# Down products of the experts in pairs: four 32-column quarters of TensorE, three buffers for down weights

## The chip, the cores and the metric

One core of a Trainium2 chip runs the whole program. The metric is the time of one execution on the device in microseconds. Three runs of the kernel before gave 1543.05, 1545.31 and 1547.57 us; their median is 1545.31 us.

## The reference, cut to what matters

The program is one inference step of a two-layer encoder on 544 rows (512 of a prompt and 32 of a sample), 1024 wide, all in fp32. Each layer is a mixer, which the change leaves alone, and then a mixture of 16 experts with hidden width 512, of which every row uses two:

```
gate = ...                               # (rows, 16), two entries of a row are not zero
for e in range(16):
    hid = silu(x @ w1[e]) * (x @ w3[e])  # up: 1024 -> 512
    y = y + gate[:, e:e+1] * (hid @ w2[e])   # down: 512 -> 1024
```

One expert's w1, w3 and w2 are 2 MiB each, so a layer reads 96 MiB of expert weights.

## The kernel before, in words

Each engine has its own instruction list, written out by hand, and semaphores order them. Per layer the rows are normalised, written to DRAM, and a router makes for every expert a list of its rows, at most 96 (`CAP`). When no expert has more than 96 rows, which is so for these inputs, the branch `own_tokens` runs on all engines:

- POOL gathers an expert's 96 rows from DRAM into one of three buffers (`own_tokens` of POOL, line 1954), three experts ahead.
- TensorE turns them (`turn_rows`, line 986: eight transposes), and DVE copies the turned rows to SBUF with the norm's gain (`own_turned`, line 1746).
- `up` (line 1001) makes both hidden products, for w1 and for w3. A stationary tile here is 64 columns of weights and the moving operand is 96 rows' worth of columns. The two 64-column halves of the array take matmuls in turn (`for o in (0, 64)`), with outputs in partitions 0 to 63 and 64 to 127 of a PSUM bank.
- ACT takes the silu (line 1275), DVE multiplies (line 1754) and writes `ghid`, of which there are two buffers.
- `down` (line 1013) multiplies with w2: the stationary tile is 96 columns of `ghid`, the moving operand 512 columns of w2. Per expert that is 2 halves of the output by 4 chunks of the contraction, 8 matmuls. Both halves of the output take PSUM banks 6 and 7.
- ACT copies both banks to `yrow` (`own_rows`, line 1282) and issues one store of 96 x 1024 to DRAM (line 1285).

An fp32 matmul stands in the trace as two MATMUL records, each with its weight load.

TensorE's order per expert is: turn the next expert's rows, `up` of expert e, `down` of expert e-1. So `down` runs one expert behind, and the last two `down` stand one after the other.

Six slots of 2 MiB hold weights: two each for w1, w3 and w2. SP issues all loads in one order (lines 582 and 592). The w1 and w3 of expert e+2 are asked for when `up` of e is done; w2 of e+2 when `down` of e is done. When the last expert's w2 has been asked for, the loads that belong to the next part (`then`: three slots of the next mixer's weights in layer 0, the final gain in layer 1) follow.

When all 16 results are in DRAM, POOL gathers each row's two results (line 1964), and DVE adds them to the stream with their gates (line 1770).

Of the kernel before, what the change touches and what calls it, by code (L numbers as in the profile page):

```python
# [12 lines left out]
P = 128  # L13
# [15 lines left out]
NE = 16  # L29
CAP = 96  # L30
# [13 lines left out]
SB_K, SB_V, SB_Q = 1, 2, 0  # L44
DF_K, DF_V, DF_Q = 4, 1, 2
OUT_EVEN, OUT_ODD = (0, 4), (0, 4)
W1, W3, W2 = (1, 3), (2, 5), (0, 4)


def tok(t):  # L50
# [182 lines left out]
def stream_kernel(nc, x_prompt, x_sample, cache_pool, cache_dsa_k, cache_dsa_v, cache_idx_k, cache_sb_k,  # L233
# [16 lines left out]
    with ctx:  # L250
# [3 lines left out]
        def sem(name):  # L254
            return ctx.enter_context(nc.semaphore(name))
# [4 lines left out]
        xT = sb("xT", [P, KC, NTOK])  # L260
        slot = sb("slot", [P, 6, 4096])
# [3 lines left out]
        arena = sb("arena", [P, 11040])  # L265
# [85 lines left out]
        xgT = arena[:, 3072:4608].rearrange("p (r k n) -> p r k n", r=2, k=KC)  # L351
        gsilu = arena[:, 4608:4992]
        ghid = arena[:, 5120:5888].rearrange("p (r m n) -> p r m n", r=2, m=4)
        yrow = arena[:, 5888:7936].rearrange("p (r d) -> p r d", r=2)
        first_y = normed[:, :].rearrange("p (t d) -> p t d", t=NT)
        second_y = arena[:, 0:5120].rearrange("p (t d) -> p t d", t=NT)

# [29 lines left out]
        bank = ctx.enter_context(nc.psum_tensor("bank", [P, 8, 512], F32))  # L387
# [16 lines left out]
        krow_in = sem("krow_in")  # L404
        vrow_in = sem("vrow_in")
        w13_in = [[sem(f"{q}_w13_in{l}") for q in ("even", "odd")] for l in range(2)]
        w2_in = [[sem(f"{q}_w2_in{l}") for q in ("even", "odd")] for l in range(2)]
        gfin_in = sem("gfin_in")
        bank_filled = sem("bank_filled")
        bank_read = {"act": sem("bank_read_act"), "dve": sem("bank_read_dve")}  # L410
# [38 lines left out]
        up_done = [sem(f"up_done{l}") for l in range(2)]  # L449
# [1 line left out]
        ghid_done = [sem(f"ghid_done{l}") for l in range(2)]  # L451
        down_done = [sem(f"down_done{l}") for l in range(2)]
        yrow_ready = [sem(f"yrow_ready{l}") for l in range(2)]
        y_stored = [[sem(f"y_stored{l}{r}") for r in range(2)] for l in range(2)]
        picked_in = [[sem(f"picked_in{l}{t}") for t in range(NT)] for l in range(2)]
        h_added = sem("h_added")
        rows_known = sem("rows_known")
# [66 lines left out]
        def _(sp):  # L524
# [60 lines left out]
            def w13_load(l, e, par):  # L585
                for w, s in ((moe_w3, W3), (moe_w1, W1)):
                    w_load(w, s[par], l, e, par)

            def w2_load(l, e, par, first=None):
                if first:  # L590
                    first(W2[par])
                sp.dma_start(slot[:, W2[par], :].rearrange("p (k n) -> p k n", k=4),
                             moe_w2[l, e].rearrange("(k p) n -> p k n", p=P)).then_inc(w2_in[l][par], 16)

            def experts(l, first, then=()):


                first(W3[0])
                w_load(moe_w3, W3[0], l, 0, 0)
                w2_load(l, 0, 0, first)  # L600
                first(W1[0])
                w_load(moe_w1, W1[0], l, 0, 0)
                first(W3[1])
                w_load(moe_w3, W3[1], l, 1, 1)
                full = crowded(sp, l)
                with sp.If(full):
                    first(W1[1])
                    w_load(moe_w1, W1[1], l, 1, 1)
                    w2_load(l, 1, 1, first)
                    with sp.Fori(0, NE // 2 - 1) as i:  # L610
                        for par in range(2):

                            sp.wait_ge(moe_y[l], (2 * i + par + 1) * NT)
                            w13_load(l, 2 * i + 2 + par, par)
                            w2_load(l, 2 * i + 2 + par, par)
                    sp.wait_ge(moe_y[l], NE * NT)
                    for load in then:
                        load()
                with sp.Else():

                    first(W1[1])
                    sp.wait_ge(xg_turned[l], 1)
                    w_load(moe_w1, W1[1], l, 1, 1)
                    w2_load(l, 1, 1, first)
                    def up_weights(e, par):

                        sp.wait_ge(up_done[l], e - 1)
                        w13_load(l, e, par)

                    def down_weights(e, par):  # L630
                        sp.wait_ge(down_done[l], e - 1)
                        w2_load(l, e, par)


                    up_weights(2, 0)
                    with sp.Fori(0, NE // 2 - 2) as i:
                        for par in range(2):
                            up_weights(2 * i + par + 3, 1 - par)
                            down_weights(2 * i + par + 2, par)
                    up_weights(NE - 1, 1)  # L640
                    down_weights(NE - 2, 0)
                    down_weights(NE - 1, 1)

                    sp.wait_ge(up_done[l], NE - 1)
                    for load in then[0:2]:
                        load()
                    sp.wait_ge(down_done[l], NE - 1)
                    for load in then[2:]:
                        load()
                    sp.wait_ge(down_done[l], NE)  # L650

            def mixer_left(layer, mech, freed):

# [71 lines left out]
        def _(pe):  # L725
# [11 lines left out]
            def weights(s, n=KC):  # L737
                return slot[:, s, :].rearrange("p (k n) -> p k n", k=n)
# [264 lines left out]
                                                        xgT[:, par, k, :], start=(k == 0), stop=(k == KC - 1))  # L1003
                last.then_inc(up_done[l], 1)

            def down(l, e, par):
                pe.wait_ge(w2_in[l][par], 16 * (e // 2) + 16)
                pe.wait_ge(ghid_done[l], e + 1)
                if e >= 1:
                    pe.wait_ge(yrow_ready[l], e)  # L1010
                for j in range(2):
                    for m in range(4):
                        last = nc.tensor.matmul(bank[0:CAP, 6 + j, :], ghid[:, par, m, :],  # L1013
                                                weights(W2[par], 4)[:, m, 512 * j:512 * j + 512],
                                                start=(m == 0), stop=(m == 3))
                last.then_inc(down_done[l], 1)

            def own_tokens(l):
                turn_rows(l, 0, 0, 0)
                for e in range(NE):  # L1020
                    if e + 1 < NE:
                        turn_rows(l, e + 1, (e + 1) % 3, (e + 1) % 2)
                    up(l, e, e % 2)
                    if e > 0:
                        down(l, e - 1, (e - 1) % 2)
                down(l, NE - 1, (NE - 1) % 2)

            def all_tokens(l):
                with pe.Fori(0, NE // 2) as i:
# [55 lines left out]
        def _(act):  # L1085
# [189 lines left out]
                nc.scalar.activation(gsilu, bank[:, 2 + 2 * (e % 2), 0:4 * CAP], ACT.Silu)\  # L1275
                  .then_inc(gsilu_done[l], 1)

            def own_rows(l, e):
                act.wait_ge(down_done[l], e + 1)
                if e >= 2:  # L1280
                    act.wait_ge(y_stored[l][e % 2], 16 * (e // 2))
                nc.scalar.copy(yrow[0:CAP, e % 2, :].rearrange("p (j n) -> p j n", j=2), bank[0:CAP, 6:8, :])\  # L1282
                  .then_inc(yrow_ready[l], 1)
                act.wait_ge(yrow_ready[l], e + 1)
                act.dma_start(y_dram[l][CAP * e:CAP * e + CAP, :], yrow[0:CAP, e % 2, :])\
                   .then_inc(y_stored[l][e % 2], 16)

            def experts(l):
                full = crowded(act, l)
                with act.If(full):  # L1290
                    all_tokens(l)
                with act.Else():
                    for e in range(NE):
                        own_silu(l, e)
                        if e > 0:
                            own_rows(l, e - 1)
                    own_rows(l, NE - 1)

            def step_u():
                for f in range(4):  # L1300
# [56 lines left out]
        def _(dve):  # L1357
# [392 lines left out]
            def own_hid(l, e):  # L1750
                dve.wait_ge(gsilu_done[l], e + 1)
                if e >= 2:
                    dve.wait_ge(down_done[l], e - 1)
                tt(ghid[:, e % 2].rearrange("p m n -> p (m n)"), gsilu,  # L1754
                   bank[:, 3 + 2 * (e % 2), 0:4 * CAP], ALU.mult).then_inc(ghid_done[l], 1)

# [70 lines left out]
        def _(pool):  # L1827
# [121 lines left out]
            def own_tokens(l):  # L1949
                all_x_stored(pool, l)  # L1950
                for e in range(NE):
                    if e >= 3:
                        pool.wait_ge(xg_turned[l], e - 2)
                    pool.indirect_dma_start(  # L1954
                        out=xg[0:CAP, e % 3, :], out_offset=None, in_=x_dram[l],
                        in_offset=bass.IndirectOffsetOnAxis(tokens_of[0:CAP, e:e + 1], 0))\
                        .then_inc(xg_in[l][e % 3], 16)

                for r in range(2):
                    pool.wait_ge(y_stored[l][r], 16 * (NE // 2))  # L1960
                pool.wait_ge(rows_known, l + 1)
                for t in range(NT):
                    for c, y in ((0, first_y), (1, second_y)):
                        pool.indirect_dma_start(
                            out=y[0:ROWS[t], t, :], out_offset=None, in_=y_dram[l],
                            in_offset=bass.IndirectOffsetOnAxis(y_rows[0:ROWS[t], NT * c + t:NT * c + t + 1], 0))\
                            .then_inc(picked_in[l][t], 16)
# [83 lines left out]
```

## Time and profile before

| what | value |
|---|---|
| median of three runs | 1545.31 us |
| the profiled execution's own time | 1546.98 us |
| its span, first to last instruction | 1545.0 us |
| TensorE (PE) busy | 1390.3 us, 90% of the span |
| weight loads of TensorE (PEld) busy | 868.2 us, 56% |
| DVE, ACT, POOL busy | 30%, 19%, 11% |
| bytes moved by DMA | 283.52 MB, 184 GB/s over the span |
| `up`, line 1001 | 352.2 us busy over both layers |
| `down`, line 1013 | 227.4 us busy over both layers |

How to read it: busy time is the union of an engine's instructions; matmuls are pipelined, so one that is recorded at 592 ns can follow the one before by less. The expert stages are at about 365 to 669 us (layer 0) and 1191 to 1498 us (layer 1) of the span. PEclk is the granted clock of TensorE as a share of 2.4 GHz; 0.50 is its lower level, 1.2 GHz. The DMA share is the mean busy share of the core's 16 DMA engines.

### The profile page before, as it was taken

Reading aid. Unit: us, or ns where it says so; the run is one execution under the profiler, and the core shown is the slowest. Engines: PE = TensorE matmul, PEld = TensorE weight load, DVE = VectorE, ACT = ScalarE, POOL = GpSimd, SP = SyncE. Lnnn points to the kernel's source line nnn. Section 1 sums busy time; section 2 is a strip of 40 time slices with the busy share of each in tenths; the row PEclk is TensorE's granted clock in tenths of the full one; section 3 lists DMA queues with packets and bytes.
Section 4 is the critical chain, followed back from the end, with each engine's and each line's share of the span. In section 5 each row is a group of like instructions: output and inputs, shape, how many; then the busy total and the mean of one; then the engine's idle time right before and its main releaser. Section 6 shows DMA issues by size and latency. Waiting matters only on the chain.

```text
span 1545.0 us, 27342 instructions
## 1 busy us (share of the span) xinstructions
PE 1390.3 (90%) x11823; PEld 868.2 (56%) x11823; DVE 467.9 (30%) x1125; ACT 288.8 (19%) x694; POOL 167.0 (11%) x216
## 2 busy tenths in 40 slices
PE   6999999987999999949999899989996999999970
PEld 3654455537777777724444444434545877777740
DVE  3047883232000000024345651245524000000007
ACT  2012333200000000012334430223210000000013
POOL 0132200001000000020112221110001000000004
PEclk8998889987999999978999899999986999999995
DMA  9300100038999999772001301021007999999834
GB/s 274 121 9 5 56 1 28 15 108 296 379 378 382 381 377 357 289 243 95 21 15 47 127 14 41 28 67 46 28 28 251 356 380 380 376 369 370 329 116 157
DMA packets 69318, 283.52 MB, mean 184 GB/s; under 512 B 19181, under 2 KB 20253, under 8 KB 61002
## 3 DMA queue, kind: packets, MB, share of 16 engines
q1 hardware_dynamic: 56190, 237.94, 41.6%
q0 software_dynamic: 9216, 31.11, 5.7%
q10 hardware_dynamic: 3788, 12.65, 2.1%
q8 instruction: 98, 1.61, 0.4%
q14 instruction: 26, 0.21, 0.0%
HBM read 257.20 MB, written 24.48 MB: 182 GB/s over the span
## 4 chain that ended last, share of the span: by engine, by line
PE 80%; DVE 8%; issue 6%; DMA 2%; POOL 1%; ACT 1%; POOLq 0%; ACTq 0%; DVEq 0%; SPq 0%
PE bank L1001 23%; PE bank L758 17%; PE bank L1013 14%; PE bank L929 9%; PE bank L854 3%; PE bank L885 3%; PE bank L986 2%; PE bank L775 2%; PE bank L863 2%; DVE h L1770 1%; PE bank L938 1%; PE bank L765 1%; POOL slot L1909 1%; DVE stats L1383 1%; DVE xT L1407 1%
## 5 line engine op out<-in xcount | busy, mean ns | idle before, releaser
L1001 PE MATMUL bank<-arena,slot 128*64 128x96 f32 x8192 | 352.2, 247 | 6.3 <-issue 5.9
L1001 PEld LDWEIGHTS bank<-arena,slot 128*64 128x64 f32 x8192 | 343.6, 138 | 13.4 <-issue 10.1
L758 PE MATMUL bank<-slot,xT 128*128 128x512 f32 (+1 forms) x640 | 302.1, 629 | 0.9 <-issue 0.9
L1013 PE MATMUL bank<-slot,arena 128*96 128x512 f32 x512 | 227.4, 597 | 2.4 <-ACT arena L1282 2.4
L758 PEld LDWEIGHTS bank<-slot,xT 128*128 128x128 f32 (+1 forms) x640 | 116.2, 187 | 161.0 <-issue 159.6
L1013 PEld LDWEIGHTS bank<-slot,arena 128*96 128x96 f32 x512 | 80.8, 163 | 126.8 <-issue 123.3
L929 PE MATMUL bank<-slot,normed 128*128 128x512 f32 (+1 forms) x320 | 148.9, 621 | 0.9 <-ACT normed L1245 0.5
L1754 DVE TENSOR_TENSOR arena<-arena,bank 128x384 f32<-128x384 f32 x32 | 17.7, 554 | 356.2 <-ACT arena L1275 356.2
L929 PEld LDWEIGHTS bank<-slot,normed 128*128 128x128 f32 (+1 forms) x320 | 57.6, 185 | 78.9 <-issue 77.6
L1746 DVE TENSOR_TENSOR arena<-bank,params 128x768 f32<-128x768 f32 x32 | 30.6, 958 | 191.2 <-PE bank L986 191.2
L854 PE MATMUL bank<-arena 64*128 64x128 f32 (+4 forms) x240 | 85.5, 498 | 3.3 <-DVE stats L1518 1.6
L1275 ACT ACTIVATE arena<-bank 128x384 f32<-128x384 f32 x32 | 15.7, 491 | 368.3 <-PE bank L1001 368.3
L885 PE MATMUL bank<-arena,slot 128*128 128x64 f32 (+5 forms) x520 | 77.7, 283 | 2.0 <-ACT slot L1184 1.0
L1954 POOL DMA_INDIRECT arena<-normed_rows,arena x32 | 29.2, 912 | 430.9 <-PE bank L986 395.6
L885 PEld LDWEIGHTS bank<-arena,slot 128*128 128x128 f32 (+2 forms) x520 | 66.6, 190 | 10.1 <-ACT slot L1184 3.7
L1282 ACT COPY arena<-bank 96x1024 f32<-96x1024 f32 x32 | 32.3, 1010 | 210.8 <-PE bank L1013 210.8
L1416 DVE TENSOR_TENSOR arena<-bank,const 128x512 f32<-128x512 f32 (+7 forms) x60 | 26.8, 494 | 145.7 <-PE bank L758 129.1
L863 PEld LDWEIGHTS bank<-const,slot 128*128 128x128 f32 (+2 forms) x260 | 27.4, 144 | 69.6 <-issue 48.2
L863 PE MATMUL bank<-const,slot 128*128 128x128 f32 (+2 forms) x260 | 49.1, 292 | 18.9 <-DVE slot L1554 8.8
L1184 ACT COPY slot<-bank 128x128 f32<-128x128 f32 (+3 forms) x80 | 33.8, 423 | 121.4 <-PE bank L863 121.4
L747 PE MATMUL bank<-const,slot 128*128 128x128 f32 (+1 forms) x160 | 25.8, 316 | 33.8 <-DVE slot L1397 33.8
L1850 POOL TENSOR_TENSOR arena<-arena 128x256 f32<-128x256 f32 (+5 forms) x60 | 33.8, 591 | 179.1 <-DVE arena L1416 103.2
(169 smaller groups left out, 1107.5 us busy)
## 6 DMA issues: line engine op xcount, KB each, us to landing
slot<-in_moe_w SPq DMA_DIRECT2D x96, 2048.0 KB, 13.4
expert_rows<-arena ACTq DMA_DIRECT2D x32, 384.0 KB, 8.5
slot<-in_w_in_odd SPq DMA_DIRECT2D x6, 2048.0 KB, 10.4
slot<-in_w_in_even SPq DMA_DIRECT2D x3, 2048.0 KB, 16.0
slot<-in_w_out_even SPq DMA_DIRECT2D x2, 2048.0 KB, 11.0
normed_rows<-slot POOLq DMA_DIRECT2D x8, 512.0 KB, 2.9
out<-arena POOLq DMA_DIRECT2D x16, 256.0 KB, 2.3
slot<-in_w_out_odd SPq DMA_DIRECT2D x2, 2048.0 KB, 8.7
```

The source lines that it names most:

```text
L758: last = nc.tensor.matmul(b[0:ROWS[t], 0:n], xT[:, k, tok(t)], w[:, k, 0:n], start=(k == 0), stop=(k == KC - 1))
L775: last = nc.tensor.matmul(b[:, :], weights(S_U)[:, k, P * f:P * f + P], xT[:, k, 0:SEQ], start=(k == 0), stop=(k == KC - 1))
L854: nc.tensor.matmul(b[0:r, 0:nk], qT[o:o + HD, tile % 2, f, 0:r], kT[o:o + HD, kf, k0:k0 + nk], start=True, stop=True)\
L863: last = nc.tensor.transpose(b[0:kr, P * i:P * i + r], prob_of(mech, n)[0:r, P * i:P * i + kr], ident[0:r, 0:r])
L885: last = nc.tensor.matmul(out[0:r, w * hd:w * hd + w], probT[0:kr, n % 2, i, 0:r], vals[0:kr, vb, c:c + w], start=(i == 0), stop=(i == len ...
L929: last = nc.tensor.matmul(b[0:ROWS[t], :], mixT[:, k, tok(t)], w[:, k % 4, 512 * j:512 * j + 512], start=(k == 0), stop=(k == KC - 1))
L986: last = nc.tensor.transpose(bank[:, k // 4, CAP * (k % 4):CAP * (k % 4) + CAP], xg[0:CAP, r3, :].rearrange("r (p k) -> r k p", k=KC)[:, k ...
L1001: last = nc.tensor.matmul(bank[o:o + 64, b, CAP * m:CAP * m + CAP], weights(w[par])[:, k, at_:at_ + 64], xgT[:, par, k, :], start=(k == 0) ...
L1013: last = nc.tensor.matmul(bank[0:CAP, 6 + j, :], ghid[:, par, m, :], weights(W2[par], 4)[:, m, 512 * j:512 * j + 512], start=(m == 0), sto ...
L1184: read(nc.scalar.copy(probT[:, n % 2, 0:nb, 0:r], b[:, 0:P * nb].rearrange("p (b n) -> p b n", b=nb)))
L1282: nc.scalar.copy(yrow[0:CAP, e % 2, :].rearrange("p (j n) -> p j n", j=2), bank[0:CAP, 6:8, :])\
L1850: last = gtt(d, x, y, op)
```

## The change

Two experts' results become twelve tiles: each expert has three tiles of 32 rows (`QUARTER` = 96/3) by two halves of 512 output columns. They are dealt to the four 32-column quarters of the array in three waves of four tiles. In a wave each quarter has a stationary tile of 32 columns of `ghid`, its own 512 columns of w2 as moving operand, and its own 32 partitions of one PSUM bank.

Two experts take three waves of 16 matmuls, 48, where they took 16. The first wave needs the first expert of the pair alone, the last the second alone. After `up` of an odd expert the pair's first wave runs, after the next `up` the other two; at the end of the stage two waves follow the first without an `up` between them. Waves alternate between banks 6 and 7.

ACT copies a wave (128 x 512) into one of four buffers and stores it in two pieces, since rows of a wave belong to different places of the result: six stores for two experts in place of two, with lines of 2 KB in place of 4 KB. `ghid` and the semaphores of `yrow` are counted by waves.

The w2 buffers become a ring of three; the third is the space of `xT`, which lies idle in this branch. SP issues w2 of expert 2 before it waits for any `up`, then w1 and w3 of e+2 after each `up` of e; after each even `up`, when the waves that read them are done, it issues the w2 loads of experts e+1 and e+2. The loop of SP is written out.

```diff
-W1, W3, W2 = (1, 3), (2, 5), (0, 4)
+W1, W3, W2 = (1, 3), (2, 5), (4, 0)
+QUARTER = CAP // 3
+WAVES = (((0, 0, 0), (0, 1, 0), (0, 2, 0), (0, 0, 1)),
+         ((0, 1, 1), (0, 2, 1), (1, 0, 0), (1, 1, 0)),
+         ((1, 2, 0), (1, 0, 1), (1, 1, 1), (1, 2, 1)))
+PIECES = (((0, 96, 0, 0, 0), (96, 128, 0, 0, 1)), ((0, 64, 0, 32, 1), (64, 128, 1, 0, 0)),
+          ((0, 32, 1, 64, 0), (32, 128, 1, 0, 1)))
+def last_wave(e):
+    return 3 * (e // 2) + 2 + e % 2
...
+                    w2_ring_load(l, 2)
+                    for e in range(NE):
+                        if e + 2 < NE:
+                            sp.wait_ge(up_done[l], e + 1)
+                            w13_load(l, e + 2, e % 2)
+                        if e >= 2 and e % 2 == 0:
+                            for done in (e - 2, e - 1):
+                                if done + 3 < NE:
+                                    sp.wait_ge(down_done[l], last_wave(done))
+                                    w2_ring_load(l, done + 3)
...
-            def down(l, e, par):
...
+            def down(l, p, part):
+                w = 3 * p + part
+                experts_of = (2 * p, 2 * p + 1)[part // 2:1 + (part + 1) // 2]
+                for e in experts_of:
+                    pe.wait_ge(w2_in[l][e % 3], 16 * (e // 3) + 16)
+                pe.wait_ge(ghid_done[l], experts_of[-1] + 1)
+                if w >= 2:
+                    pe.wait_ge(yrow_ready[l], w - 1)
+                for m in range(4):
+                    for c, (q, third, j) in enumerate(WAVES[part]):
+                        w2 = w2_ring[(2 * p + q) % 3].rearrange("p (k n) -> p k n", k=4)
+                        last = nc.tensor.matmul(bank[QUARTER * c:QUARTER * c + QUARTER, 6 + w % 2, :],
+                                                ghid[:, q, m, QUARTER * third:QUARTER * third + QUARTER],
+                                                w2[:, m, 512 * j:512 * j + 512], start=(m == 0), stop=(m == 3))
+                last.then_inc(down_done[l], 1)
...
-                    if e > 0:
-                        down(l, e - 1, (e - 1) % 2)
-                down(l, NE - 1, (NE - 1) % 2)
+                    if e % 2:
+                        down(l, e // 2, 0)
+                    elif e > 0:
+                        down(l, e // 2 - 1, 1)
+                        down(l, e // 2 - 1, 2)
+                down(l, NE // 2 - 1, 1)
+                down(l, NE // 2 - 1, 2)
...
+            def own_rows(l, p, part):
+                w = 3 * p + part
+                act.wait_ge(down_done[l], w + 1)
+                if w >= 4:
+                    act.wait_ge(y_stored[l][w % 4], 32 * (w // 4))
+                nc.scalar.copy(yrow[:, w % 4, :], bank[:, 6 + w % 2, :]).then_inc(yrow_ready[l], 1)
+                act.wait_ge(yrow_ready[l], w + 1)
+                for lo_, hi_, q, row, j in PIECES[part]:
+                    row += CAP * (2 * p + q)
+                    act.dma_start(y_dram[l][row:row + hi_ - lo_, 512 * j:512 * j + 512], yrow[lo_:hi_, w % 4, :])\
+                       .then_inc(y_stored[l][w % 4], 16)
...
             def own_hid(l, e):
                 if e >= 2:
-                    dve.wait_ge(down_done[l], e - 1)
+                    dve.wait_ge(down_done[l], last_wave(e - 2))
```

## Rows read from the trace of the kernel before

**Rows 1.** The page: the span, and DMA busy tenths in 40 slices of it.
```profile
span 1545.0 us, 27342 instructions
...
DMA  9300100038999999772001301021007999999834
```

**Rows 2.** Windows: bounds, length, busy PE, PEld, DVE, ACT, POOL, clock, DMA share, GB/s.
```profile
394.20:630.60 236.40, 235.35 (x3527) 179.15 (x3527) 19.10 (x25) 19.02 (x25) 9.07 (x10) 1.00 0.98 376
...
630.60:668.70 38.10, 36.68 (x416) 22.61 (x412) 1.63 (x7) 3.02 (x5) 0.00 (x0) 1.00 0.78 281
...
1221.20:1458.50 237.30, 236.33 (x3532) 179.75 (x3532) 19.11 (x25) 19.02 (x25) 9.07 (x10) 1.00 0.98 376
1458.50:1497.50 39.00, 36.80 (x412) 22.54 (x406) 1.11 (x2) 3.03 (x5) 0.00 (x0) 1.00 0.37 134
```

**Rows 3.** Waits in layer 0's expert stage: engine, line, for whom, total, times, longest.
```profile
PE bank L1013 <- ACT arena L1282: 1.2, 1, 1.2
...
SPq L582 <- PE bank L1001: 160.9, 14, 15.7
SPq L592 <- PE bank L1013: 93.5, 14, 18.6
```

**Rows 4.** Groups by line, 378.4 to 668.7 us: shapes, count, busy us, mean ns, idle before.
```profile
L1001 PE MATMUL bank<-arena,slot 128*64 128x96 f32 x3842 | 163.9, 247 | 1.6 <-issue 1.3
...
L1013 PE MATMUL bank<-slot,arena 128*96 128x512 f32 x256 | 113.7, 597 | 1.2 <-ACT arena L1282 1.2
...
L1282 ACT COPY arena<-bank 96x1024 f32<-96x1024 f32 x16 | 16.2, 1009 | 105.4 <-PE bank L1013 105.4
...
L986 PE MATMUL bank<-const,arena 96*128 96x96 f32 x112 | 14.4, 272 | 0.0
```

**Rows 5.** Timeline of layer 0: first and last two `down`, and the last copy.
```profile
390.75 7.11 PE L1013 MATMUL bank<-slot,arena 128*96 128x512 f32 x16
...
653.27 7.11 PE L1013 MATMUL bank<-slot,arena 128*96 128x512 f32 x16
...
661.57 7.08 PE L1013 MATMUL bank<-slot,arena 128*96 128x512 f32 x16 [1.19 <-ACT arena L1282]
...
668.68 1.01 ACT L1282 COPY arena<-bank 96x1024 f32<-96x1024 f32 x1 [7.26 <-PE bank L1013]
```

**Rows 6.** The page's DMA queues (packets, MB, share) and issues (KB, us to landing).
```profile
q1 hardware_dynamic: 56190, 237.94, 41.6%
...
q10 hardware_dynamic: 3788, 12.65, 2.1%
...
slot<-in_moe_w SPq DMA_DIRECT2D x96, 2048.0 KB, 13.4
expert_rows<-arena ACTq DMA_DIRECT2D x32, 384.0 KB, 8.5
```

**Rows 7.** Two issue times in layer 0, w13 of expert 2 and of 15.
```profile
L582 SPq DMA_DIRECT2D slot<-in_moe_w x1: 432/432/432, 378.9 to 378.9; - x1
...
DMA to landing us min/median/max: 15.4/15.4/15.4
...
L582 SPq DMA_DIRECT2D slot<-in_moe_w x2: 338/382/426, 616.6 to 617.0; - x2
...
DMA to landing us min/median/max: 8.2/10.9/13.6
```

**Rows 8.** Windows of 20 to 40 ns at the start of one `up`: PE and PEld instructions.
```profile
642.54:642.58 0.04, 0.02 (x2) 0.02 (x2) 1.00 0.00 0
...
642.66:642.68 0.02, 0.02 (x2) 0.02 (x4) 1.00 0.00 0
642.68:642.70 0.02, 0.02 (x4) 0.02 (x5) 1.00 0.00 0
```

**Rows 9.** A wait of TensorE early in layer 1's mixer, and the window that follows.
```profile
718.70 1.08 PE L747 MATMUL bank<-const,slot 32*128 32x32 f32 x8 [2.90 <-DVE slot L1397]
...
718.00:728.00 10.00, 8.62 (x24) 5.20 (x25) 3.79 (x8) 1.80 (x4) 0.00 (x0) 0.50 0.78 268
```

More of the change, by code:

```diff
@@ L353, in stream_kernel @@
         ghid = arena[:, 5120:5888].rearrange("p (r m n) -> p r m n", r=2, m=4)
-        yrow = arena[:, 5888:7936].rearrange("p (r d) -> p r d", r=2)
+        yrow = arena[:, 5888:7936].rearrange("p (r d) -> p r d", r=4)
+        w2_ring = (slot[:, W2[0], :], slot[:, W2[1], :], xT[:, :, :].rearrange("p k n -> p (k n)")[:, 0:4096])
         first_y = normed[:, :].rearrange("p (t d) -> p t d", t=NT)
@@ L406, in stream_kernel @@
         w13_in = [[sem(f"{q}_w13_in{l}") for q in ("even", "odd")] for l in range(2)]
-        w2_in = [[sem(f"{q}_w2_in{l}") for q in ("even", "odd")] for l in range(2)]
+        w2_in = [[sem(f"w2_in{l}{r}") for r in range(3)] for l in range(2)]
         gfin_in = sem("gfin_in")
@@ L453, in stream_kernel @@
         yrow_ready = [sem(f"yrow_ready{l}") for l in range(2)]
-        y_stored = [[sem(f"y_stored{l}{r}") for r in range(2)] for l in range(2)]
+        y_stored = [[sem(f"y_stored{l}{r}") for r in range(4)] for l in range(2)]
         picked_in = [[sem(f"picked_in{l}{t}") for t in range(NT)] for l in range(2)]
@@ L593, in w2_load, with w2_ring_load @@
                              moe_w2[l, e].rearrange("(k p) n -> p k n", p=P)).then_inc(w2_in[l][par], 16)
+            def w2_ring_load(l, e):
+                sp.dma_start(w2_ring[e % 3].rearrange("p (k n) -> p k n", k=4),
+                             moe_w2[l, e].rearrange("(k p) n -> p k n", p=P)).then_inc(w2_in[l][e % 3], 16)
             def experts(l, first, then=()):
@@ L624, in experts @@
                     w2_load(l, 1, 1, first)
[L625 to L642, printed above, removed]
+                    w2_ring_load(l, 2)
[8 more added lines that the diff above has]
+                                    w2_ring_load(l, done + 3)
                     sp.wait_ge(up_done[l], NE - 1)
@@ L646, in experts @@
                         load()
-                    sp.wait_ge(down_done[l], NE - 1)
+                    sp.wait_ge(down_done[l], last_wave(NE - 3))
                     for load in then[2:]:
                         load()
-                    sp.wait_ge(down_done[l], NE)
+                    sp.wait_ge(down_done[l], last_wave(NE - 1))
             def mixer_left(layer, mech, freed):
@@ L1004, in up @@
                 last.then_inc(up_done[l], 1)
-            def down(l, e, par):
[L1007 to L1015, printed above, removed]
+            def down(l, p, part):
[12 more added lines that the diff above has]
+                                                w2[:, m, 512 * j:512 * j + 512], start=(m == 0), stop=(m == 3))
                 last.then_inc(down_done[l], 1)
@@ L1276, in own_silu @@
                   .then_inc(gsilu_done[l], 1)
[L1278 to L1286, printed above, removed]
+            def own_rows(l, p, part):
[9 more added lines that the diff above has]
+                       .then_inc(y_stored[l][w % 4], 16)
             def experts(l):
@@ L1294, in experts @@
                         own_silu(l, e)
-                        if e > 0:
-                            own_rows(l, e - 1)
-                    own_rows(l, NE - 1)
+                        if e % 2:
+                            own_rows(l, e // 2, 0)
+                        elif e > 0:
+                            own_rows(l, e // 2 - 1, 1)
+                            own_rows(l, e // 2 - 1, 2)
+                    own_rows(l, NE // 2 - 1, 1)
+                    own_rows(l, NE // 2 - 1, 2)
             def step_u():
@@ L1957, in own_tokens @@
                         .then_inc(xg_in[l][e % 3], 16)
-                for r in range(2):
-                    pool.wait_ge(y_stored[l][r], 16 * (NE // 2))
+                for r in range(4):
+                    pool.wait_ge(y_stored[l][r], 32 * (3 * NE // 2 // 4))
                 pool.wait_ge(rows_known, l + 1)
```

## Prediction

> **What bounds the kernel now.** I read the page first. Two stretches of the span have the DMA engines at nine tenths and more, slice after slice [rows 1]: the expert stages, and the change touches nothing else. The windows show what is special there. From the landing of expert 2's w1 and w3 to that of expert 15's, layer 0 takes 236.4 us and layer 1 237.3 us; in both TensorE is busy all the time at its upper clock level (1.00, 2.4 GHz), and the DMA engines are busy 0.98 of it at 376 GB/s [rows 2]. So two resources are nearly full at once, and the waits tell which one sets the pace: in the whole stage TensorE waits 1.2 us for another engine, once, and never for a load, while SP waits 160.9 us for `up` and 93.5 us for `down` before it may ask for the next weights [rows 3]. TensorE is the bound, with DMA right behind it.
>
> How far behind? TensorE per expert: `down` begins at 390.75 for expert 0 and at 653.27 for expert 14, 14 periods, 18.75 us each [rows 5]. The parts: 3842 records of `up` are 15 experts of 256, 163.9/15 = 10.9 us; 16 records of `down` in 7.11 us with the last one's tail; a record lasts 592 ns but the next starts after (7.11 - 0.592)/15 = 0.434 us, say 0.43, so 16 x 0.43 = 6.9 us; turning 14.4/14 = 1.0 us [rows 4, 5]. Sum 18.8 us.
>
> DMA per expert: three weights of 2048 KB, a store of 384 KB [rows 6] and a gather of as much, 6912 KB = 7.08 MB. At 376/0.98 = 384 GB/s that is 18.4 us. So only 0.4 us per expert is to be had before the loads take over.
>
> **The change part by part.** *Waves.* A pair has 48 matmuls, 96 records, where it had 32 records. If the four quarters work at once, it takes 96/4 x 0.43 = 10.3 us, 3.43 us a wave, in place of 13.7 us: 1.7 us less per expert, and TensorE alone would need 17.1 us. Do they work at once? No row shows four. The nearest are the halves of `up`: two records begin together, some 0.13 us later the next two [rows 8], and 256 records take 10.9 us, 43 ns each, where 96 columns at the 0.43 us per 512 of `down` would take 80 ns alone. So two streams run at full rate, from the first record on, both passes of an fp32 product side by side with the neighbour's. Bounds from both sides: four at once 3.43 us a wave, two at once 6.9 us, none 13.7 us. I take four, since two show a loss of only 2 x 43 - 80 = 6 ns a step.
>
> *The Trainium skill's word on it.* "TensorE: Matmul & The Clock Gate", section "Measured speedup vs the span model", gives 2.38 times for three column tiles and 3.07 for four row tiles. No run here shows either. By 3.07 a wave would take 32 x 0.43/3.07 = 4.5 us and a pair 13.4 us, 0.16 us less per expert: with the wait of 1.2 us that goes, 3.8 us per stage and 1538 for the whole. The first rival below is its mechanism, priced without it.
>
> *The pace after.* At 17.1 us TensorE is ahead of 18.4 us of DMA, so the loads set the pace and `up` of the last expert begins when its weights land. In layer 0 w1 of expert 2 lands at 378.9 + 15.4 = 394.3, that of expert 15 at 617.0 + 13.6 = 630.6 [rows 7]; between them lie the same bytes after as before. Ahead of the first now stands w2 of expert 2, issued early: 2.1 MB at 384 GB/s, 5.5 us. Of the 0.02 x 236.4 = 4.7 us in which DMA idled about 3 are taken up, since TensorE releases buffers sooner. So the last w1 lands at 630.6 + 5.5 - 3 = 633, and after it come 10.9 us of `up`, three waves of 3.43 and 0.3 us of starts: 654.4. Before, the last `down` ended at 661.57 + 7.08 = 668.65 [rows 5]. Gain 14.3 us. Layer 1 repeats it: bounds 1221.2 and 1458.5 [rows 2], 1458.5 + 5.5 - 3 + 21.5 = 1482.5 against 1497.5, gain 15.0. Together 29.3 us. Half of it is the tail: after the last weights TensorE has 10.3 us of waves to do where it had two `down`, the second after a wait of 1.19 us for the copy [rows 5]; waves alternate between two banks, so that wait is gone.
>
> *Third buffer and order on SP.* It moves w2 loads earlier and adds no bytes. The new waits for two waves after an even `up` hold SP 6.9 us; behind them stand only w2 of e+1 and e+2, needed an `up` or more later, and then the wait for the next `up`, 11 us away. So nothing on the path. In layer 0 the next mixer's third load is no longer issued after the last but one `down`; it lands sooner, at no gain I count, because the stores and gathers after the stage wait for results.
>
> *Copies and stores.* ACT has three copies of 512 columns per pair for two of 1024 (1009 ns each) and six issues for two; it idles 105.4 us before its copies in the stage [rows 4], so nothing. `ghid` is written later by up to two waves, and read an `up` later. Stores in lines of 2 KB: by the queues' rows a packet costs 0.416 x 1545 x 16/56190 = 0.183 us at 4.2 KB on q1 and 0.021 x 1545 x 16/3788 = 0.137 us at 3.3 KB on q10 [rows 6], so cost goes with bytes. If it went with packets instead, the stores' 2.1% would double: 32 us over both stages, on the bound. Near zero by the nearer reading; I take 0.5 us per stage. The other way, the last store is smaller (256 KB in place of 384) and its copy shorter: up to 0.7 us per stage, left out.
>
> *New waits on TensorE.* After the first wave, `up` of expert 2 waits for its weights: the wave ends at 390.75 + 3.4 = 394.2, the weights land at 394.3 + 5.5 = 399.8. That is 5.6 us, and later ones of up to 2 x (18.4 - 17.1) = 2.6 us per pair. In the mixer a wait of 2.90 us stood just before 10.0 us at the lower level (0.50, 1.2 GHz) [rows 9]. Ten microseconds at half pace cost 5 us of TensorE's time, and they delay the release of buffers, with DMA's queue short of work at that very point. From both sides: nothing (waits of 1.2 us in the stage left the clock at 1.00), or a fall in each stage with its 5 us and another before the last `up`, 10 us. I take 2.5 us per stage.
>
> Sum: 1546.98 (the profiled execution's own time, span 1545.0 and 2.0 around it) - 29.3 + 1.0 + 5.0 = 1523.7. The median of the runs shown is 1.7 us under that execution, so 1522.
>
> **The rivals.** *The quarters hold back each other, three at work on average.* For: no row has four streams, and a wave reads four moving operands where `up` reads one. Against: two lose 6 ns. A wave is then 32 x 0.43/3 = 4.6 us, a pair 13.7 us as before; TensorE stays the bound and only the one wait of 1.2 us per stage goes: 2.4 us, 1543. (From 3.2 quarters on, 12.9 us a pair, TensorE is level with the loads and the forecast holds with a tail longer by up to 2.6 us a stage.)
>
> *Slower: only two quarters run at a time.* Three waves of 6.9 us are 20.6 us for a pair in place of 13.7, 3.4 us more per expert; TensorE at 22.2 us is then the bound, the loads wait for it, and 2 x (16 x 3.43 - 1.2) = 107 us are added: 1653. This decides as soon as fewer than 3 quarters are at work on average, since 48 matmuls stand for 16. For it: the array is shown to do two, with one moving operand for both halves, and no row shows a third tile at work. Against: the pair of records begins at once at the first step, so nothing in the order of passes holds the second tile back.
>
> *DMA does not set the pace.* If loads went faster than 384 GB/s, as nothing shows, TensorE's saving would come through whole: 2 x (16 x 1.7 + 1.2) = 57 us, 1488.
>
> *The change does nothing:* pace and tail both stay with the loads, as when DMA loses by idling between a late release and the next load what the tail gains (14 us a stage). Two waits like the first with a fall of the clock each would do it. 1545.
>
> **How the numbers follow.** The forecast with its own range, 1508 to 1533 (the 10 us of clock per stage above, no clock cost and faster tails below): 0.70. About three quarters: 0.10. Two quarters: 0.11. TensorE's whole saving: 0.04. Nothing gained: 0.05. For eight in ten the range reaches from 1505 to 1544, which takes in three quarters and leaves out the other three rivals. Faster by over 0.3% (4.6 us, about what a measurement of this kernel tells from no change): the first, a third of the second, the fourth: 0.78. Within: the rest of the second and most of the fifth, 0.11. Slower: two quarters, 0.11.
>
> **What would show it.** Right: the span of one wave is near 3.4 us; TensorE waits for loads before `up`, some 5 us at expert 2 and a few at later ones; SP's waits shrink; the DMA share stays at 0.97 or more up to the last weights; from the landing of the last w1 to the end of the last wave 21 to 22 us. Wrong: waves of 4.5 us or more with no waits for loads (quarters that hold back each other); a clock at 0.50 inside the stage (then the wait has a price); a DMA share well under 0.97 with TensorE waiting (then order and buffers on SP are at fault, not the bytes).

## The result and the profile after

The changed kernel takes 1504.57 us (median of four runs, 1499.62 to 1508.59), the kernel before beside it 1545.32 us: a ratio of 0.973 with a 95% interval of 0.9711 to 0.9748. It is faster by 41 us. The forecast was 1522 with a range from 1505 to 1544: right in its sign and wrong in its size, and the median lies 0.4 us under the range.

The span was cut into its four parts: stage of layer 0 (first `up` to last `down`), what lies up to the next first `up`, stage of layer 1, the end. Columns as in [rows 2]. First the kernel before, then the changed one:

```profile
364.60:668.60 304.00, 299.44 (x4465) 226.35 (x4464) 23.75 (x36) 23.00 (x31) 10.88 (x12) 1.00 0.95 360
668.60:1193.10 524.50, 463.12 (x1623) 232.75 (x1622) 224.56 (x545) 144.82 (x376) 76.42 (x99) 0.88 0.19 66
1193.10:1497.40 304.30, 300.20 (x4465) 227.10 (x4464) 23.21 (x31) 23.01 (x31) 10.88 (x12) 1.00 0.91 342
1497.40:1545.00 47.60, 0.04 (x1) 0.00 (x0) 27.18 (x30) 16.17 (x27) 22.44 (x15) 0.52 0.42 149
```

```profile
span 1497.8 us, 29356 instructions
...
366.80:647.80 281.00, 274.29 (x4977) 208.28 (x4976) 23.76 (x36) 21.34 (x39) 10.81 (x12) 1.00 1.00 389
647.80:1168.20 520.40, 458.76 (x1625) 230.81 (x1622) 224.51 (x545) 144.42 (x376) 76.10 (x99) 0.89 0.19 67
1168.20:1451.10 282.90, 276.88 (x4977) 210.51 (x4976) 23.20 (x31) 21.34 (x39) 10.86 (x12) 0.99 0.95 368
1451.10:1497.80 46.70, 0.01 (x3) 0.00 (x0) 27.18 (x30) 15.73 (x27) 22.14 (x15) 0.54 0.41 149
```

The stages lost 23.0 and 21.4 us, 44.4 together, where the forecast's terms for them made 23.3 (29.3 - 1.0 - 5.0). The part between them is 4.1 us shorter in this execution and the stage of layer 0 begins 2.2 us later. The profiled execution is the fastest of its four (1499.62 us); another, shown in the experiments, has stages of 280.6 and 281.7 us and 525.3 us between them. So the stages are the gain, and the rest differs from run to run.

The lines that answer to [rows 2] are the windows between the landings of w1 of expert 2 and of expert 15:

```profile
399.90:625.20 225.30, 222.73 (x4055) 169.09 (x4056) 19.66 (x26) 17.53 (x32) 9.01 (x10) 1.00 0.99 392
625.20:647.80 22.60, 22.60 (x368) 13.87 (x360) 1.08 (x6) 2.25 (x4) 0.00 (x0) 1.00 1.03 386
1200.60:1428.50 227.90, 224.88 (x4053) 171.19 (x4057) 18.70 (x25) 17.52 (x32) 8.14 (x9) 0.99 0.99 388
1428.50:1451.10 22.60, 22.60 (x368) 13.87 (x360) 0.55 (x1) 2.25 (x4) 0.00 (x0) 1.00 0.45 160
```

The reader is to see that the same loads passed in 225.3 and 227.9 us instead of 236.4 and 237.3, at 392 and 388 GB/s. The forecast had taken 384 GB/s as all that the engines can do.

The timeline of TensorE, layer 0 (start, length, records): a single wave, the last `up` and the beginning of the last waves.

```profile
604.25 3.64 PE L1028 MATMUL bank<-slot,arena 128*32 128x512 f32 x32
607.82 1.13 PE L997 MATMUL bank<-const,arena 96*128 96x96 f32 x8
...
619.60 7.07 PE L1028 MATMUL bank<-slot,arena 128*32 128x512 f32 x64
626.60 10.78 PE L1012 MATMUL bank<-arena,slot 128*64 128x96 f32 x256
```

A wave of 32 records follows at 3.57 us (604.25 to 607.82), two waves at 7.00 (619.60 to 626.60); before, 16 records took 6.9 us [rows 5]. Four quarters are at work. The weights of expert 15 land at 604.7 + 20.4 = 625.1, 1.5 us before its `up`:

```profile
L597 SPq DMA_DIRECT2D slot<-in_moe_w x2: 340/684/1027, 604.4 to 604.7; - x2
...
DMA to landing us min/median/max: 15.4/17.9/20.4
```

The waits of layer 0 [rows 3] and, in the last three lines, of TensorE in layer 1:

```profile
PE bank L1012 <- issue: 4.9, 6, 2.3
...
SPq L597 <- PE bank L1012: 187.8, 14, 15.7
SPq L611 <- PE bank L1028: 52.4, 13, 17.5
...
PE bank L1012 <- DMA slot<-in_moe_w: 3.4, 3, 1.9
PE bank L1028 <- issue: 1.7, 3, 0.6
PE bank L1012 <- issue: 0.9, 2, 0.5
```

In layer 0 TensorE still waits for no load; SP still waits 187.8 us for `up`. In layer 1 it waits 3.4 us for them. But for that, the loads came as fast as TensorE used them.

### The profile page after: what moved, and what is told of

It is laid out like the page before. It is cut to its first block, busy times and chain, and to the rows that moved or that the text cites. A ratio compares the mean times of both kernels' runs of the same rounds, so it can differ in the third digit from the quotient of the medians.

```text
span 1497.8 us, 29356 instructions
## 1 busy us (share of the span) xinstructions
PE 1341.6 (90%) x12847; PEld 834.2 (56%) x12847; DVE 467.8 (31%) x1125; ACT 284.5 (19%) x710; POOL 166.3 (11%) x216
## 4 chain that ended last, share of the span: by engine, by line
PE 75%; DVE 9%; DMA 7%; issue 6%; POOL 2%; ACT 1%; ACTq 0%; POOLq 0%; SPq 0%; DVEq 0%
PE bank L1012 21%; PE bank L769 18%; PE bank L940 10%; PE bank L1028 10%; DMA slot<-in_moe_w 5%; PE bank L865 3%; PE bank L896 3%; PE bank L786 2%; PE bank L874 2%; PE bank L997 2%; DVE h L1795 1%; PE bank L949 1%; POOL slot L1934 1%; DVE stats L1408 1%; PE bank L776 1%
## 5 line engine op out<-in xcount | busy, mean ns | idle before, releaser
L1779 DVE TENSOR_TENSOR arena<-arena,bank 128x384 f32<-128x384 f32 x32 | 17.7, 554 | 401.7 <-ACT arena L1294 203.1
L1028 PE MATMUL bank<-slot,arena 128*32 128x512 f32 x1056 | 137.5, 594 | 1.7 <-issue 1.7
L1028 PEld LDWEIGHTS bank<-slot,arena 128*32 128x32 f32 x1056 | 36.9, 110 | 71.3 <-issue 69.0
L896 PEld LDWEIGHTS bank<-arena,slot 128*128 128x128 f32 (+2 forms) x520 | 67.8, 193 | 10.3 <-ACT slot L1203 3.9
L1028 PE MATMUL bank<-xT,arena 128*32 128x512 f32 x480 | 71.6, 594 | 0.0
L874 PE MATMUL bank<-const,slot 128*128 128x128 f32 (+2 forms) x260 | 50.3, 297 | 18.4 <-DVE slot L1579 8.8
L1302 ACT COPY arena<-bank 128x512 f32<-128x512 f32 x48 | 28.1, 586 | 148.2 <-PE bank L1028 148.2
```

The source lines that it names most:

```text
L874: last = nc.tensor.transpose(b[0:kr, P * i:P * i + r], prob_of(mech, n)[0:r, P * i:P * i + kr], ident[0:r, 0:r])
L896: last = nc.tensor.matmul(out[0:r, w * hd:w * hd + w], probT[0:kr, n % 2, i, 0:r], vals[0:kr, vb, c:c + w], start=(i == 0), stop=(i == len ...
L1028: last = nc.tensor.matmul(bank[QUARTER * c:QUARTER * c + QUARTER, 6 + w % 2, :], ghid[:, q, m, QUARTER * third:QUARTER * third + QUARTER], ...
```

## The experiments

Three theories say why the stages gained almost twice what was forecast. **Demand**: the 376 GB/s of the kernel before were what TensorE's 18.75 us per expert asked for, and the engines can do more in either kernel. **Depth**: 384 GB/s was the limit of the old order, and the third buffer raised it by keeping more loads queued. **The record, repaired** (C in the expectations): the loads set the pace of the changed kernel, at 396 GB/s. In the first expectations demand is A and depth is B.

### The limit of the loads, in either order

Both kernels with `up` cut to half of its contraction, so that TensorE has far less to do than the loads (one run each, as with the light loads and the exchanged loops below; the readings are from windows of their traces):

```diff
-                        for k in range(KC):
+                        for k in range(KC // 2):
                             for o in (0, 64):
...
-                                                        xgT[:, par, k, :], start=(k == 0), stop=(k == KC - 1))
+                                                        xgT[:, par, k, :], start=(k == 0), stop=(k == KC // 2 - 1))
```

> The kernel before, with up contracting over 512 of its 1024 inputs (half of up's matmuls left out, so the result is not the reference's). TensorE needs 5.4 + 1.0 + 6.9 = 13.3 us per expert, and the loads, 7.08 MB per expert in the old order with two buffers each, must set the pace. Theory A (demand): the 376 GB/s of the kernel before were what TensorE's 18.75 us per expert asked for, and the engines can do more: over 395 GB/s in the steady part, 16.5 to 17.9 us per expert, stage 265 to 288 us instead of 304, whole 1470 to 1515. Theory B (depth): the old order holds the engines at 384 GB/s or less: 18.4 us per expert or more, stage 298 to 304, whole 1535 to 1545.

> The changed kernel with the same cut of up (half of its contraction left out). TensorE needs 5.4 + 1.0 + 5.1 = 11.5 us per expert, so the loads set the pace with the ring of three and the new order. Theory A (demand): the same rate as the cut kernel before, within 2%, over 395 GB/s, and the stage falls below the 281 us of the changed kernel to 262 to 278. Theory B (depth): 396 to 410 GB/s here and 384 or less in the cut kernel before. The theory of the record in its repaired form (C: loads set the pace of the changed kernel, only at 396 instead of 384): the stage stays at 278 to 283 us less half an up (5 us) at its end.

Windows of the steady part, layers 0 and 1, and TensorE's waits in layer 0, of the cut kernel before:

```profile
407.00:578.00 171.00, 142.32 (x1515) 96.13 (x1514) 15.04 (x20) 15.00 (x20) 8.10 (x9) 0.93 1.02 401
1203.00:1374.00 171.00, 142.95 (x1519) 96.47 (x1518) 15.12 (x20) 15.00 (x20) 8.13 (x9) 0.94 1.02 403
...
PE bank L1001 <- DMA slot<-in_moe_w: 27.1, 13, 5.9
PE bank L1013 <- DMA slot<-in_moe_w: 13.5, 8, 2.6
```

The same windows of the cut changed kernel:

```profile
406.00:581.00 175.00, 134.91 (x1946) 90.64 (x1946) 15.68 (x21) 14.76 (x27) 8.14 (x9) 0.86 1.01 396
1207.00:1380.00 173.00, 134.03 (x1932) 90.85 (x1932) 15.12 (x20) 14.18 (x26) 8.13 (x9) 0.86 1.01 398
...
PE bank L1012 <- DMA slot<-in_moe_w: 69.2, 8, 15.6
```

Now TensorE does wait for loads in both, and the old order with two buffers moves 401 and 403 GB/s, no less than the ring's 396 and 398. Depth falls as the reason for a limit of 384; demand is borne out. The cut kernels took 1482.5 and 1488.3 us, stages of 271.0 and 270.8, 274.7 and 272.6 us. At 401 GB/s an expert's 7.08 MB take 17.7 us. That is the number that should have stood for 18.4. It is a rate reached, not a limit proven: in the cut kernel before, SP still waited 106.5 us for `up` and 107.0 for `down` in layer 0.

The repaired record does not fall here. It had the stage at 278 to 283 us less 5 for the half `up` at its end, 273 to 278, and 274.7 lies inside, 272.6 just under. Of the 6.3 and 10.3 us that the changed kernel's stages lose by the cut, 5.4 are that half `up`.

### What the loads still cost in the changed kernel

The changed kernel without w3 of expert 2 and later (`up` reads the first two experts' w3 again):

```diff
-                            w13_load(l, e + 2, e % 2)
+                            w_load(moe_w1, W1[e % 2], l, e + 2, e % 2)
...
-                pe.wait_ge(w13_in[l][par], 32 * (e // 2) + 32)
+                pe.wait_ge(w13_in[l][par], 16 * (e // 2) + 32)
```

> The changed kernel without the loads of w3 from expert 2 on (up reads the first two experts' w3 again, so the result is not the reference's): 4.98 MB per expert in place of 7.08. TensorE's own phases of a stage sum to 16 x 10.7 + 15 x 1.06 + 24 x 3.43 = 269.4 us, against 281.0 and 282.9 us measured. A: TensorE is the bound and its 11 to 13 us of standing are mostly not waits for loads (the code of the program, the lower clock at the start): stage 273 to 279, whole 1488 to 1500. C: the loads set the pace: stage 269 to 271, whole at most 1480.

Steady windows of both layers, and below them one of the uncut changed kernel:

```profile
407.00:584.00 177.00, 177.00 (x3228) 134.29 (x3228) 15.12 (x20) 14.20 (x26) 8.13 (x9) 1.00 0.77 284
1208.00:1382.00 174.00, 174.00 (x3174) 132.09 (x3174) 15.12 (x20) 14.19 (x26) 8.15 (x9) 1.00 0.78 288
...
407.00:588.00 181.00, 178.43 (x3236) 135.10 (x3234) 15.12 (x20) 14.20 (x26) 8.12 (x9) 1.00 1.01 395
```

1490.8 us, stages of 276.8 and 274.2 us: inside what A expected there (TensorE is the bound), and not the 269 to 271 of C. With a third fewer weight bytes a stage loses only 4 to 9 us, and with half of `up` gone it loses 1 to 5 beyond that half `up`. So neither sets the pace by much: in the changed kernel TensorE and the loads are about level. The loads run at 395 GB/s, about the 396 and 398 of its cut version. They are a little slower than TensorE (17.7 us and more per expert against about 17.1) and live on a lead, which shrinks: by the issue and landing times in layer 0 the weights of expert 5 land 3.4 us before its `up`, those of expert 11 1.0 us, those of expert 15 1.5 us.

In layer 0 no wait for a load is shown, and yet TensorE stands still for 2.6 of the 181 us, in short stops that wait for no engine ("issue"), and for none of the 177 us with light loads. The stops go with the full loads; what they wait for, the traces do not show.

### The changed kernel again

> The changed kernel once more, for a second trace and its spread (1499.6 to 1508.6 before now). All theories 1504 +- 5. Its stages 281 to 286 us; if the runs differ by how fast the loads go, a slower run shows waits for loads before up at a DMA rate under 396 GB/s (C in part), and otherwise the difference stands in the mixers.

1503.7 us, ratio 0.9732 (0.9705 to 0.9759), stages 280.6 and 281.7. Against the first trace it is the part between the stages that differs, 525.3 and 520.4 us, and not the loads. A third time, as a neighbour of the last two experiments:

> The changed kernel beside these two on the same chip: 1504 +- 3, stages 280 to 283 us.

1503.9 us, stages 283.5 and 282.4. Over the three traces the two stages together are 42.4 to 46.0 us shorter than in the kernel before.

### The parts of the change, one at a time

The third buffer and its order on SP with the old `down`:

```diff
+                    w2_ring_load(l, 2)
+                    for e in range(NE):
+                        if e + 2 < NE:
+                            sp.wait_ge(up_done[l], e + 1)
+                            w13_load(l, e + 2, e % 2)
+                        if e >= 1 and e + 2 < NE:
+                            sp.wait_ge(down_done[l], e)
+                            w2_ring_load(l, e + 2)
```

> The kernel before with the third buffer for down weights and SP's order that goes with it (w2 of expert 2 at the start, then w2 of e+2 after down of e-1), but with the 96-row tiles of down and whole stores. Theory A (demand) and B (depth) alike: TensorE stays the bound at 18.75 us per expert, so 1542 to 1547, and the DMA rate stays at 376 to 378 GB/s, since 7.08 MB per 18.75 us are asked for. If the third buffer had a gain by itself it would be under 1540.

1546.7 us, ratio 1.0007 (0.9992 to 1.0021); 380 GB/s at the old period. Nothing, as TensorE is the bound there. The other way round, the waves with two buffers:

```diff
-                    w2_ring_load(l, 2)
...
-                                if done + 3 < NE:
+                                if done + 2 < NE:
                                     sp.wait_ge(down_done[l], last_wave(done))
-                                    w2_ring_load(l, done + 3)
+                                    w2_ring_load(l, done + 2)
```

> The changed kernel with two buffers for down weights: w2 of e and e+1 are asked for after the two waves that follow an even up. w2 of e then lands at the earliest 2 + 11 + 5.5 = 18.5 us after that up, and its wave needs it 7 + 1 + 10.7 = 18.7 us after it. Theory A: the engines are fast enough, the time rises by 0 to 8 us to 1504 to 1512. Theory B: with less queued the rate falls back to 376 to 384 GB/s, expert period 18.4 to 18.8 us, 1520 to 1535.

1538.4 us, ratio 0.9951 (0.9929 to 0.9973): only 8 us of the 41 are left, worse than either theory. Its window in layer 0 and TensorE's wait there:

```profile
407.00:607.00 200.00, 185.01 (x3218) 135.64 (x3222) 15.41 (x21) 14.53 (x27) 8.13 (x9) 0.97 0.92 360
...
PE bank L1027 <- DMA slot<-in_moe_w: 16.3, 6, 3.8
```

The expectation had seen that w2 of an even expert would land just when its wave needs it (18.5 against 18.7 us), which leaves 0.2 us for any delay ahead of it in the queue. It came late six times, by up to 3.8 us. TensorE waits 16.3 us, the mean granted clock of the window is 0.97 instead of 1.00, and the DMA engines are busy 0.92 of it. Here they are slow because too little is asked for at a time, not because they can do no more: with the third buffer they did 392. So the third buffer, with the order that it allows, is worth nothing alone and some 34 us together with the waves. (The run also issues the next mixer's third load later, but the loss stands in the stages: 300.3 and 298.4 us, against 281.0 and 282.9.)

### Order within a wave

Both inner loops exchanged, quarter outside and chunk inside:

```diff
-                for m in range(4):
-                    for c, (q, third, j) in enumerate(WAVES[part]):
+                for c, (q, third, j) in enumerate(WAVES[part]):
+                    for m in range(4):
```

> The changed kernel with the two inner loops of a wave exchanged: each quarter runs its four chunks one after the other, then the next quarter. If matmuls start in program order and a quarter takes one at a time, the quarters then overlap only at their borders: 13 steps of 2 x 0.43 = 0.86 us, 11.2 us a wave in place of 3.43; 24 waves in 2 stages, at most 2 x 24 x 7.8 = 372 us more, about 1860 to 1880. If TensorE took later quarters' matmuls ahead of waiting ones, it would stay at 1504.

1718.4 us. A wave on the timeline, and in windows:

```profile
445.27 8.86 PE L1028 MATMUL bank<-xT,arena 128*32 128x512 f32 x32
454.06 1.13 PE L997 MATMUL bank<-const,arena 96*128 96x96 f32 x8
...
445.27:447.00 1.73, 1.73 (x4) 0.47 (x5) 1.00 0.68 142
447.00:452.20 5.20, 5.20 (x25) 1.59 (x24) 1.00 0.93 384
452.20:454.06 1.86, 1.86 (x6) 0.33 (x3) 1.00 1.01 432
```

8.79 us to the next work instead of 3.57, neither the 11.2 us of strict order nor full freedom, so the expected 1860 to 1880 missed as 1504 did. The last three lines are windows of this wave (a record that reaches over a border counts in both). In the first 1.73 us 4 records run, one per 0.43 us: one quarter alone. In the next 5.20 us there are two per 0.43 us, and in the end one again. That fits a quarter that begins when the one before it is half done. Why no earlier, the runs do not show. It is near the forecast's slower rival, two quarters at a time (6.9 us a wave), in another kernel.

### Attempts at a faster one

```diff
-                    w2_ring_load(l, 2)
                     for e in range(NE):
                         if e + 2 < NE:
                             sp.wait_ge(up_done[l], e + 1)
                             w13_load(l, e + 2, e % 2)
+                        if e == 0:
+                            w2_ring_load(l, 2)
```

> The changed kernel with w2 of expert 2 asked for after w1 and w3 of expert 2 instead of ahead of them. In layer 1 of the changed kernel up of expert 2 waited for its weights; that wait (3.4 us of waits for loads in the stage, 2.1 of them there) should go, in layer 0 up to 2 us. A: 1 to 5 us less than the changed kernel, 1499 to 1503. C (loads set the pace throughout): no change, since the bytes until the last weights are the same, 1504 +- 2.

1505.5 us (1500.6 to 1505.9), no gain: the expectation of 1 to 5 us missed. The wait at expert 2 went, and waits of 2.4 us for loads came in layer 0 before `up`.

```diff
                     first(W1[1])
-                    sp.wait_ge(xg_turned[l], 1)
                     w_load(moe_w1, W1[1], l, 1, 1)
+                    sp.wait_ge(xg_turned[l], 1)
                     w2_load(l, 1, 1, first)
                     w2_ring_load(l, 2)
```

> The changed kernel with w1 of expert 1 asked for right behind w1 of expert 0, ahead of the wait for the first turned rows, in a stretch where the DMA engines were at 0.15 (5 us). If loads pace the stage in part (the light loads took 4 to 8 us off a stage), 2 MB moved 16 us earlier put every later load 5 us earlier: 2 to 5 us less per stage, less up to 3 us for slower gathers of the first rows: 1494 to 1503. If TensorE alone paces it: no change or up to 6 us more through the gathers, 1504 to 1510.

And with the wait gone altogether from SP:

> The same with w2 of experts 1 and 2 ahead of that wait too: 6 MB queued while the first rows are gathered. Their landing then shares the engines with 16 us of loads: up of expert 0 starts 5 to 10 us later, and from then on nothing waits for loads. If loads pace the stage: 1500 to 1512; if TensorE alone: 1514 to 1524.

1507.9 us (1506.2 to 1511.5) and 1512.2 us (1508.0 to 1513.5), with the changed kernel beside them at 1503.9 (1501.5 to 1505.9): slower by the runs, though the intervals of the ratios, 0.9719 to 0.9786, 0.9732 to 0.9804 and 0.9683 to 0.9750, overlap. The first gain expected (1494 to 1503) did not come, and the second run lies between its two expectations. The first rows come later: TensorE's longest wait for their gather in layer 0 grows from 6.7 us in the changed kernel to 12.8 with w1 of expert 1 moved,

```profile
PE bank L997 <- DMA arena<-normed_rows,arena: 12.8, 1, 12.8
```

while the stages shorten by at most 4.6 us against the neighbour (278.9 and 281.0, then 280.4 and 281.2 beside 283.5 and 282.4). No version here beats the changed kernel.

## Why the prediction was wrong

*What bounds the kernel before: right.* TensorE, with no waits for loads; the ring alone changes nothing and the light loads little.

*The waves: right.* 3.43 us were forecast; alone they take 3.57 to the next work, in twos 3.50. What the rest is was not tried. A pair takes 10.57 us (3.57 + 7.00) against 13.7 us before; those 13.7 us are 16 products one after another, 3.8 to 3.9 times a wave of 16. The Trainium skill ("TensorE: Matmul & The Clock Gate", section "Measured speedup vs the span model") has no row for four column tiles alone; by its 3.07 times for four row tiles a wave would be an estimated 4.5 us. The trace does not bear that out here.

*DMA per expert, "At 376/0.98 = 384 GB/s that is 18.4 us": this is the step that failed.* A rate was divided by a busy share as if 1.00 were the engines' limit. But 7.08 MB per 18.75 us are 378 GB/s: the rate was TensorE's own demand. With TensorE's work cut, the same loads went at 401 to 403 GB/s, 17.7 us per expert. And the share does not measure what is left: 376 at 0.98 in the kernel before, 401 to 403 at 1.02 in the cut one, 360 at 0.92 with two buffers, 284 at 0.77 with light loads, so 369 to 395 GB/s per unit of share. [Rows 3] had the sign of it: SP waited 160.9 us for `up`, TensorE never for a load. A resource whose client never waits has not shown its limit. The Trainium skill ("DMA: Bandwidth & Descriptors", section "Where 436 GB/s comes from") puts the ceiling of a core's 16 ports at 435 GB/s. The changed kernel's trace has 436 in one stretch of 5 us with no gather or store in it, so it agrees as an upper end:

```profile
350.00:355.00 5.00, 4.84 (x27) 4.68 (x27) 2.25 (x6) 0.00 (x0) 0.00 (x0) 0.50 1.02 436
```

The same section names about 358 GB/s per core as what binds between HBM and SBUF. The 401 to 403 measured here, with one core at work, are above that, and the measurement decides.

The size of the error by this step: 233.2 us were forecast between the two landings in layer 0 (399.8 to 633) and 234.3 in layer 1, and they took 225.3 and 227.9: 7.9 + 6.4 = 14.3 us. With 396 GB/s in place of 384 the forecast's own step would have given 226.1 and 227.2. So the term was mis-sized; that the loads run at full rate between the two landings was right, and that they alone set the pace there was not quite, since TensorE is level with them.

*The tail after the last weights: 21.5 us forecast, 22.6 measured in both layers*, 2.2 us too little over both, since TensorE was not waiting for the last weights but 1.4 to 1.5 us behind them.

*The waits and the clock: priced too high.* 2.5 us per stage were taken. In layer 0 expert 2's weights land when TensorE comes to them anyway (399.9, after a stop of 2.3 us within `up` of expert 1 that waits for no engine), and no wait for a load follows. In layer 1 it waits 1.9 us, and 3.4 us at the lower level come behind it:

```profile
1198.00:1201.80 3.80, 1.87 (x35) 1.70 (x36) 0.96 (x1) 0.29 (x1) 0.90 (x1) 1.00 0.99 415
1201.80:1205.20 3.40, 3.40 (x48) 3.40 (x46) 0.00 (x0) 0.00 (x0) 0.00 (x0) 0.50 1.05 393
```

Half pace for 3.4 us is 1.7 us of lost time, in place of the 5.0 taken for both stages. With two buffers, where TensorE waits 16.3 us in layer 0, the clock fell more (0.97 over 200 us).

*Stores in pieces:* 1.0 us was taken; the runs cannot separate it. The queue's share rose from 2.1% to 2.4% for twice the packets, and not to 4.2%:

```profile
q10 hardware_dynamic: 7884, 12.65, 2.4%
```

*The third buffer, "moves w2 loads earlier and adds no bytes":* no price was put on it, and it is what the gain hangs on: without it 8 of the 41 us are left. The sum took for granted that no load is asked for too late, and that held only with the third buffer.

Sum: between the landings 14.3 us less than forecast, up to the first of them 3.3 less (33.1 and 32.4 us from the first `up`, forecast 35.2 and 33.6), behind the last 2.2 more: 15.4. These stretches hold whatever clock and stores cost, so the 6.0 us added for the two go as well: 21.4, against 44.4 - 23.3 = 21.1 measured. Two of the forecast's sums are off in the last digit (633.1 + 21.5 is 654.6, not 654.4; the chances of faster add up to 0.77, not 0.78), which changes nothing. The rival "DMA does not set the pace" (1488, chance 0.04) had the rate right, loads faster than 384 GB/s, and was dismissed with "as nothing shows". It was not right as a whole: 57 us were possible by its sum and 44 came in the stages. With light loads the two stages are 57.3 us shorter than before (304.0 + 304.3 - 276.8 - 274.2), so TensorE's saving is there, and the full loads keep 13 us of it.

## What to carry to other kernels

A transfer rate in a stage where the engine never waits for its loads is that engine's demand, not the limit of the loads; to learn the limit, cut the engine's work in half and look again, before a sum rests on it. Two edits can each be worth little alone (here 0 and 8 us) and 41 together, because one speeds the consumer and the other keeps the loads asked for in time. In tiled matmuls try the loop over tiles innermost: the same 16 products of a wave took 3.57 or 8.8 us by the order of two loops.

## What the runs showed of the hardware that was not expected

Four 32-column quarters of TensorE with four different fp32 moving operands ran at the full rate of each: 32 records in 3.5 us, 0.43 us per step of four. With the quarters' chunks in a row it kept two quarters at work in the middle of a wave and one at its ends. The DMA busy share was 1.02 over 171 us (1.05 in one stretch of 3.4 us) and is no measure of the room left (369 to 395 GB/s per unit of it in the steady windows).
